# Two zero columns between prompt and sample tokens in the recurrent block

## The reference, cut to what matters

```
gate_br, x_br = split(h @ w_in)
xc  = conv4(x_br)                     # per feature: taps at t-1, t, t+1, t+2, zero outside the sequence
r, gi = sigmoid(xc @ w_a + b_a), sigmoid(xc @ w_i + b_i)     # block diagonal, 10 blocks of 128; two directions
a = exp(-8 r softplus(-lam));  u = sqrt(1 - a*a) * gi * xc
y_t = a_t * y_(t-1) + u_t             # a scan forwards and one backwards; the sample starts from a given state
out = ((y_fwd + y_bwd) * gelu(gate_br)) @ w_out
```

## Time and profile before

| what | us |
|---|---|
| median of 3 runs | 1550.23 (1549.12 to 1550.41) |
| the profiled execution, own time | 1546.95 |
| its span, first to last instruction | 1545.3 |
| PE busy in the span | 1509.9 (98%) |
| DVE busy | 1128.7 (73%) |
| ACT busy | 660.2 (43%) |
| GpSimd busy | 138.8 (9%) |

### The profile page before, as it was taken

How to read it: one execution, slowest core, us unless ns; L and a number is a source line. 1 busy time by engine, 2 the same in 40 slices (tenths; PEclk the granted TensorE clock), 3 DMA queues, 4 the chain that set the end, 5 groups by cost and what they waited for, 6 DMA issues and landing times.

```text
span 1545.3 us, 25482 instructions
## 1 busy us (share of the span) xinstructions
PE 1509.9 (98%) x9222; PEld 1482.9 (96%) x9222; DVE 1128.7 (73%) x1757; ACT 660.2 (43%) x953; POOL 138.8 (9%) x212
## 2 busy tenths in 40 slices
PE   8999999999979999999999999999999999999998
PEld 7999999989979999999999999998779999999998
DVE  4898888879987877789887777986997575344342
ACT  5533342369955333332343333225555553333321
POOL 0010000000120000001000000000642000000000
PEclk9999999999989999999999999999999999999999
DMA  9666666513432655667555556753222134334421
GB/s 375 232 234 220 229 246 223 193 56 118 142 109 96 219 192 187 205 216 243 165 183 184 192 190 215 254 194 114 69 82 89 49 109 150 124 134 137 150 94 41
DMA packets 68282, 257.08 MB, mean 166 GB/s; under 512 B 7585, under 2 KB 8609, under 8 KB 67969
## 3 DMA queue, kind: packets, MB, share of 16 engines
q1 hardware_dynamic: 48944, 187.57, 35.9%
q0 software_dynamic: 18512, 67.58, 13.0%
q10 hardware_dynamic: 768, 1.19, 0.2%
HBM read 253.68 MB, written 2.63 MB: 166 GB/s over the span
## 4 chain that ended last, share of the span: by engine, by line
PE 87%; DVE 7%; ACT 3%; issue 2%; DMA 0%; POOL 0%; DVEq 0%; SPq 0%; ACTq 0%
PE bank L570 25%; PE bank L572 25%; PE bank L571 25%; DVE tmp_a L1576 2%; DVE h_lo L1595 1%; DVE w_lo_sb L1488 1%; ACT w_hi_sb L1019 1%; PE wide L872 1%; PE bank L583 1%; PE bank L649 1%; DVE bcum L2062 0%; PE bank L894 0%; DVE wide L1507 0%; PE wide L681 0%; PE bank L693 0%
## 5 line engine op out<-in xcount | busy, mean ns | idle before, releaser
L1019 ACT ACTIVATE w_hi_sb<-raw 128x1024 fp32r<-128x1024 f32 (+3 forms) x308 | 344.1, 1122 | 476.6 <-PE bank L572 451.7
L570 PE MATMUL bank<-h_hi,w_hi_sb 128*128 128x384 f32 x1567 | 530.0, 338 | 3.4 <-DVE tmp_a L1700 1.3
L1488 DVE TENSOR_TENSOR w_lo_sb<-raw,w_hi_sb 128x1024 fp32r<-128x1024 f32 (+3 forms) x308 | 402.2, 1307 | 172.6 <-ACT w_hi_sb L1019 169.9
L571 PE MATMUL bank<-h_lo,w_hi_sb 128*128 128x384 f32 x1567 | 527.5, 337 | 0.0
L572 PE MATMUL bank<-h_hi,w_lo_sb 128*128 128x384 f32 x1567 | 527.4, 337 | 0.0
L570 PEld LDWEIGHTS bank<-h_hi,w_hi_sb 128*128 128x128 f32 x1567 | 295.4, 189 | 7.8 <-DVE w_lo_sb L1488 2.8
L572 PEld LDWEIGHTS bank<-h_hi,w_lo_sb 128*128 128x128 f32 x1567 | 295.3, 188 | 0.0
L571 PEld LDWEIGHTS bank<-h_lo,w_hi_sb 128*128 128x128 f32 x1567 | 295.2, 188 | 0.0
L570 PE MATMUL bank<-a_hi,w_hi_sb 128*128 128x384 f32 x704 | 236.9, 336 | 1.5 <-DVE a_lo L1711 1.5
L572 PE MATMUL bank<-a_hi,w_lo_sb 128*128 128x384 f32 x704 | 236.6, 336 | 0.0
L571 PE MATMUL bank<-a_lo,w_hi_sb 128*128 128x384 f32 x704 | 236.6, 336 | 0.0
(11 more groups left out here) (321 smaller groups left out, 1575.1 us busy)
## 6 DMA issues: line engine op xcount, KB each, us to landing
raw<-in_ffn_in SPq DMA_DIRECT2D x176, 512.0 KB, 3.6
ada_raw<-in_ada_w POOLq DMA_DIRECT2D x128, 512.0 KB, 3.5
raw<-in_ffn_out SPq DMA_DIRECT2D x64, 704.0 KB, 4.3
raw<-in_rg_in SPq DMA_DIRECT2D x20, 512.0 KB, 3.3
ada_first<-in_ada_w SPq DMA_DIRECT2D x8, 1024.0 KB, 17.5
raw<-in_rg_out SPq DMA_DIRECT2D x8, 640.0 KB, 3.8
raw<-in_gla_qk SPq DMA_DIRECT2D x8, 512.0 KB, 3.6
raw<-in_gla_v SPq DMA_DIRECT2D x8, 512.0 KB, 3.3
```

The source lines that it names most:

```text
L570: pe.matmul(out, w_hi_sb[:, slot, w], hi[k], start=start and j == 0, stop=False)
L571: pe.matmul(out, w_hi_sb[:, slot, w], lo[k], start=False, stop=False)
L1019: A(w_hi_sb[:, s, 0:w], raw[:, s, 0:w], ACT.Copy).then_inc(w_hi, 1)
L1488: V.tensor_tensor(w_lo_sb[:, s, 0:w], raw[:, s, 0:w], w_hi_sb[:, s, 0:w].bitcast(F32), ALU.subtract).then_inc(w_split, 1)
```

## The change

In the recurrent stage alone, every buffer has 386 columns in place of 384: two columns stand between the prompt and the sample, and they are zero in the input of the stage. The sample begins at column 130. Each tap is one DVE instruction over 385 or 384 columns, with the border inside the sample included; the zero columns stand for the zeros outside the sequences, and L1826 is gone. All matmuls, ACT and DVE steps of the stage, the output product among them, have two columns more. The norm writes its result to `hg_hi` and `hg_lo` (rows of 386), which GpSimd clears in the gap ahead of the stage; PE waits for that (`gap_cleared`). To make room, `rgc` lies where `reset` is, and `reset` is filled after the stage, behind GpSimd's `low_y`, instead of at the start of the program.

```diff
+GAP = 2
+TG = T + GAP
...
+        rg_slots = sb("rg_slots", [P, 4, 2, TG], F32, slot_scope)
...
+        hg_hi = sb("hg_hi", [P, DC, TG], F32R, hg_scope)
+        hg_lo = sb("hg_lo", [P, DC, TG], F32R, hg_scope)
...
+        rgc_scope = ExitStack()
+        rgc = sb("rgc", [P, 12, 2 * RC], F32, rgc_scope)
+        rgc_scope.close()
         reset = sb("reset", [P, T], F32, ctx)
...
-            pool.memset(reset[:, :], 1.0).then_inc(consts, 1)
-            pool.wait_ge(consts, 3)
-            pool.memset(reset[:, :].rearrange("p (n t) -> p n t", t=P)[:, :, 0:1], 0.0).then_inc(consts, 1)
...
                 if f == 0:
+                    pool.wait_ge(masks_made, 1)
+                    pool.memset(hg_hi[:, :, TP:TP + GAP].bitcast(F32), 0.0).then_inc(gap_cleared, 1)
+                    pool.memset(hg_lo[:, :, TP:TP + GAP].bitcast(F32), 0.0).then_inc(gap_cleared, 1)
                     for m in range(RC):
                         low_y(m)
+                    pool.wait_ge(gate_read, 4 * RC)
+                    pool.memset(reset[:, :], 1.0).then_inc(consts, 1)
+                    pool.wait_ge(consts, 3)
+                    pool.memset(reset[:, :].rearrange("p (n t) -> p n t", t=P)[:, :, 0:1], 0.0).then_inc(consts, 1)
...
-            arriving(base, range(DC), h_chunks, hhi_ready, h_ready, DC, DC - 1, bank, RING - 1)
+            pe.wait_ge(gap_cleared, 2)
+            arriving(base, range(DC), hg_chunks, hhi_ready, h_ready, DC, DC - 1, bank, RING - 1, TG)
...
-                tile(bank[out][:, 0:T], n % RING, range(DC), *h_chunks, True, True).then_inc(w_used, 1)
+                tile(bank[out][:, 0:TG], n % RING, range(DC), *hg_chunks, True, True).then_inc(w_used, 1)
...
-                out, ps = xc[:, m % 4, :], bank[X_BANK[m]][:, 0:T]
-                out3, ps3 = (v.rearrange("p (a b) -> p a b", a=NT) for v in (out, ps))
+                out, ps = xc[:, m % 4, :], bank[X_BANK[m]][:, 0:TG]
                 for k in (0, 2, 3):
                     s = k - 1
                     w = conv_w[:, m, k:k + 1]
-                    to, fr = (slice(1, P), slice(0, P - 1)) if s < 0 else (slice(0, P - s), slice(s, P))
-                    V.scalar_tensor_tensor(out3[:, :, to], ps3[:, :, fr], w, out3[:, :, to], ALU.mult, ALU.add)
-                    to = slice(2 * P, 2 * P + 1) if s < 0 else slice(2 * P - s, 2 * P)
-                    fr = slice(2 * P - 1, 2 * P) if s < 0 else slice(2 * P, 2 * P + s)
+                    to, fr = (slice(1, TG), slice(0, TG - 1)) if s < 0 else (slice(0, TG - s), slice(s, TG))
                     last = V.scalar_tensor_tensor(out[:, to], ps[:, fr], w, out[:, to], ALU.mult, ALU.add)
```

More of the change, by code:

```diff
@@ L193, in build @@
         hbuf_scope.close()
+        hg_scope = ExitStack()
+        hg_hi = sb("hg_hi", [P, DC, TG], F32R, hg_scope)
+        hg_lo = sb("hg_lo", [P, DC, TG], F32R, hg_scope)
+        rg_scope = ExitStack()
+        gate = sb("gate", [P, RC, TG], F32, rg_scope)
+        y32 = sb("y32", [P, RC, TG], F32, rg_scope)
+        xc = sb("xc", [P, 4, TG], F32, rg_scope)
+        xc_hi = sb("xc_hi", [P, 3, TG], F32R, rg_scope)
+        xc_lo = sb("xc_lo", [P, 3, TG], F32R, rg_scope)
+        rgs = sb("rgs", [P, 7, 2, TG], F32, rg_scope)
+        rg_scope.close()
+        rgy_scope = ExitStack()
+        y_hi = sb("y_hi", [P, RC, TG], F32R, rgy_scope)
+        y_lo = sb("y_lo", [P, RC, TG], F32R, rgy_scope)
+        rgy_scope.close()
+        hg_scope.close()
         out_scope = ExitStack()
@@ L198, in build @@
         mask_in = y_out[:, :, :].rearrange("p m t -> p (m t)")[:, 0:NLEV * P]
-        sb("span_all", [P, 2 * DC * T + 2 * FC * T], F32, ctx)
+        sb("span_all", [P, 2 * DC * T + 2 * FC * T + 2 * P], F32, ctx)
         extra = sb("extra", [P, 2 * D], F32, ctx)
         crow = extra[:, :].rearrange("p (c k) -> p c k", c=2)
-        a_slot = [rgs[:, j, :, :] for j in range(3)] + [tmp_a[:, :, :]]
-        s_slot = [rgs[:, j, :, :] for j in range(3, 6)] + [tmp_b[:, :, :]]
-        u_slot = [rgs[:, 6, :, :]] + [scr[:, j:j + 2, :] for j in (0, 2)]
+        a_slot = [rgs[:, j, :, :] for j in range(3)] + [rg_slots[:, 0, :, :]]
+        s_slot = [rgs[:, j, :, :] for j in range(3, 6)] + [rg_slots[:, 1, :, :]]
+        u_slot = [rgs[:, 6, :, :]] + [rg_slots[:, j, :, :] for j in (2, 3)]
         pst = extra[:, 0:2 * DV].rearrange("p (a b) -> p a b", a=2)
@@ L387, in col_major, with h_out, at_of @@
             return ap
+        def h_out(q):
+            return (hg_hi, hg_lo) if q == 1 else (h_hi, h_lo)
+        def at_of(q, g, t0):
+            return t0 + GAP if q == 1 and g else t0
         def row_major(ap, q, n):
@@ L576, in _ @@
             h_chunks = ([h_hi[:, k, :] for k in range(DC)], [h_lo[:, k, :] for k in range(DC)])
+            hg_chunks = ([hg_hi[:, k, :] for k in range(DC)], [hg_lo[:, k, :] for k in range(DC)])
             a_chunks = ([a_hi[:, k, :] for k in range(FC)], [a_lo[:, k, :] for k in range(FC)])
@@ L633, in norm, with arriving @@
                     keep_busy(6)
-            def arriving(base, ks, chunks, hi_ready, ready, n0, early=5, bank=bank, together=RING):
+            def arriving(base, ks, chunks, hi_ready, ready, n0, early=5, bank=bank, together=RING, width=T):
                 for b in range(together):
@@ L644, in arriving @@
                     for b in range(together):
-                        pe.matmul(bank[b][:, 0:T], w_hi_sb[:, b, w], chunks[0][k], start=k == 0, stop=False)
-                        pe.matmul(bank[b][:, 0:T], w_lo_sb[:, b, w], chunks[0][k], start=False, stop=False)
+                        pe.matmul(bank[b][:, 0:width], w_hi_sb[:, b, w], chunks[0][k], start=k == 0, stop=False)
+                        pe.matmul(bank[b][:, 0:width], w_lo_sb[:, b, w], chunks[0][k], start=False, stop=False)
                     pe.wait_ge(ready, n0 + k + 1)
                     for b in range(together):
-                        pe.matmul(bank[b][:, 0:T], w_hi_sb[:, b, w], chunks[1][k], start=False, stop=False)
+                        pe.matmul(bank[b][:, 0:width], w_hi_sb[:, b, w], chunks[1][k], start=False, stop=False)
                 pe.wait_ge(ready, n0 + len(ks))
                 for b in range(together):
-                    tile(bank[b][:, 0:T], b, ks[early:], *chunks, False, True, early).then_inc(w_used, 1)
+                    tile(bank[b][:, 0:width], b, ks[early:], *chunks, False, True, early).then_inc(w_used, 1)
                 for b in range(together, RING):
                     pe.wait_ge(w_split, base + b + 1)
-                    tile(bank[b][:, 0:T], b, ks, *chunks, True, True).then_inc(w_used, 1)
+                    tile(bank[b][:, 0:width], b, ks, *chunks, True, True).then_inc(w_used, 1)
             def one_tile_blocks(name, chunks, ks, hi_ready, ready, n0, early=5, together=RING):
@@ L789, in _ @@
             pe.wait_ge(rg_p, RC)
-            arriving(base, range(RC), y_chunks, rg_yhi, rg_yready, 0, RC - 2, bank[4:8])
+            arriving(base, range(RC), y_chunks, rg_yhi, rg_yready, 0, RC - 2, bank[4:8], width=TG)
             pe.wait_ge(gelu_ready, RC)
@@ L793, in _ @@
                 pe.wait_ge(w_split, base + b + 1)
-                tile(bank[b - RING][:, 0:T], b % RING, range(RC), *y_chunks, True, True).then_inc(w_used, 1)
+                tile(bank[b - RING][:, 0:TG], b % RING, range(RC), *y_chunks, True, True).then_inc(w_used, 1)
             ffn(1, 2)
@@ L1236, in centre_tap @@
                     act.wait_ge(rg_p, m - 3)
-                A(xc[:, m % 4, :], bank[X_BANK[m]][:, 0:T], ACT.Identity, bias=conv_b[:, m:m + 1],
+                A(xc[:, m % 4, :], bank[X_BANK[m]][:, 0:TG], ACT.Identity, bias=conv_b[:, m:m + 1],
                   scale=conv_w[:, m, 1:2]).then_inc(tap_ready, 1)
@@ L1254, in gates @@
                     act.wait_ge(gate_done, GATES_BEFORE[m] + dr + 1)
-                    A(bank[6 + dr][:, 0:T], bank[6 + dr][:, 0:T], ACT.Tanh, bias=rgc[:, 0, col[dr]],
+                    A(bank[6 + dr][:, 0:TG], bank[6 + dr][:, 0:TG], ACT.Tanh, bias=rgc[:, 0, col[dr]],
                       scale=0.5).then_inc(tanh_a, 1)
@@ L1261, in gates @@
                         act.wait_ge(gate_done, GATES_BEFORE[m] + 3 + dr)
-                    A(bank[4 + dr][:, 0:T], bank[4 + dr][:, 0:T], ACT.Tanh, bias=rgc[:, 1, col[dr]],
+                    A(bank[4 + dr][:, 0:TG], bank[4 + dr][:, 0:TG], ACT.Tanh, bias=rgc[:, 1, col[dr]],
                       scale=0.5).then_inc(tanh_i, 1)
@@ L1279, in gelu @@
                 act.wait_ge(w_used, base + RG_AT["b", m] + 1)
-                A(gate[:, m, :], bank[B_BANK[m]][:, 0:T], ACT.Gelu_apprx_tanh).then_inc(gelu_ready, 1)
+                A(gate[:, m, :], bank[B_BANK[m]][:, 0:TG], ACT.Gelu_apprx_tanh).then_inc(gelu_ready, 1)
             def high_y(m):
@@ L1860, in from_state @@
                 dve.wait_ge(rg_u, m + 1)
[L1861 to L1862 removed]
+                at = slice(TP + GAP, TP + GAP + 1)
+                V.scalar_tensor_tensor(u[:, 0, at], a[:, 0, at], h0[:, 0, m:m + 1],
```

(1 more changed line is left out.)

43 lines of the change are left out of this document (18 added, 25 removed).

## The result

The changed kernel takes 1571.72 us (median of 4 runs, 1569.53 to 1573.45); the kernel before, on the same chip, 1549.67 us (4 runs, 1546.84 to 1550.41). The ratio is 1.0151, 95% interval 1.0138 to 1.0163. The time is far above the range of the forecast, and the profiled executions differ as much: 1569.53 us after, 1546.95 before.

What follows compares the result with a forecast made beforehand. The prediction took PE to bound the recurrent stage until about 389 us and from 437, ACT between, with DVE's saving hidden. Terms 0.37 + 0.10 + 0.02 + 0.22 = +0.7 us gave 1550.9 us, range 1549.0 to 1554.0.

Steps and rivals of the forecast that it cites:

- the change part by part: Section costing taps, PE's and ACT's two columns, GpSimd and the tail of the recurrent stage; sum +0.7 us.
- The sum: Recurrent stage: 0.37 + 0.10 + 0.02 + 0.22 = +0.7 us, giving 1550.9 us for the median.
- one paragraph alone: Stage rows of 1544 bytes cross more 16-byte lines; at a supposed 1% on 636 PE matmuls, 1.1 us more.
- The rival that came nearest: PE in the recurrent stage: 386 columns cost like a fuller width, 1559.8 us; chance 0.13, including a like price on ACT.
- point of decision: PE's odd-width rival decides from 4.9 ns a matmul on (3.1 us over 636), a pace of 178.2 ns.
- signs of being wrong: 386-column pace over 178 ns, an ACT step grown by more than a few ns, or output product 2 us or more early.
- DVE hidden: Recurrent stage: DVE ends some 3.3 us freer, hidden behind ACT and PE, so the saving counts as 0.
- ACT: small: ACT between 389 and 436 us: two more columns cost 1.8 ns a step, 0.10 us in all.
- PE's columns: Recurrent stage matmuls: two columns cost 0.93 ns each, 0.37 us up to 389 us and 0.22 in the output product.
- the slope between two widths: PE's 384 columns at 173.3 ns and 512 at 232.9 give 0.466 ns a column, used to price 386.
- GpSimd: right: Gap clears before the stage are covered by some 15 us; filling `reset` after `low_y` delays nothing: 0.

Runs made afterwards that it cites:

- with the shift taken out: The changed kernel without its two unused 64-byte buffers (gap, rgc_gap), so activations begin 1024 bytes lower than in the kernel before: 1551.92 us, ratio 1.0018.
- Taking the repairs out by themselves: The kernel before without the 30 steps (L1826) that mend the convolution's border columns, at its own addresses and 384 columns: 1548.55 us, ratio 1.0000.

## Why the prediction was wrong

**The step that failed** is in the change part by part: the diff's allocations were costed as work (clears, loads, what queues behind them) and never as places. The sum has no term outside the recurrent stage, which takes for granted that a matmul that the diff doesn't touch keeps its 173.3 ns. It did not: the 6936 of this width outside the stage went to 176.7, for some 19 of the 22 us. The layout was looked at in one paragraph alone, and there only at row starts inside the stage, with a weight of 1.1 us. The 1% behind that weight is the prediction's own supposition and not from the page: the Trainium skill (SBUF — State Buffer, Specifications) names a penalty for a crossed line and no size of it. By the lines of 16 bytes that it gives, every such row, not every second one, would touch one line more.

**The rival that came nearest** was PE paying for the new layout, and it had the wrong mechanism: it laid the price on 386 columns, and set its point of decision at 178.2 ns. The pace in the stage stayed below that, 177.8 ns on `hg_hi` after (143 matmuls, start to start) and 176.3 with the shift taken out. The slowness was of 384-column matmuls elsewhere, which none of its signs of being wrong would have caught.

The other terms, read in the change with its shift taken out where the shift would blur them:

*DVE hidden: right.* The taps are steps of 616 and 619 ns, no L1826 is left, and a block takes 1.84 us (1.83 forecast). DVE by line and shape, after, the answer to the earlier trace rows:

```profile
L1848 DVE SCALAR_TENSOR_TENSOR xc<-bank,small,xc 128x385 f32<-128x385 f32 x20 | 12.3, 616 | 3.2 <-ACT xc L1261 2.9
...
L1848 DVE SCALAR_TENSOR_TENSOR xc<-bank,small,xc 128x384 f32<-128x384 f32 x10 | 6.2, 619 | 0.3
```

and its timeline, block 0, the answer to the earlier trace rows: the third tap is over and the weight block begins at 333.52 - 331.68 = 1.84.

```profile
331.68 1.93 DVE L1848 SCALAR_TENSOR_TENSOR xc<-bank,small,xc 128x385 f32<-128x385 f32 x3 [1.66 <-ACT xc L1261]
333.52 1.22 DVE L1512 TENSOR_TENSOR w_lo_sb<-raw,w_hi_sb 128x1024 fp32r<-128x1024 f32 x1
```

DVE's busy time in the stage fell by 147.72 - 144.58 = 3.1 us (3.3 forecast), and ACT's waits from 389 to 437 us still name PE alone in their counterparts after (0.7, 0.4 and 0.4 us, by the earlier trace rows 0.7, 0.4, 0.2). Taking the repairs out by themselves gained nothing that can be measured.

*ACT: small, as forecast.* By line and shape its gate steps went from 693 to 696 and from 686 to 690 ns, its own step of the convolution from 675 to 679; 1.8 ns each was forecast, 3 to 4 came, some 0.1 us more over 57 steps.

*PE's columns: the size was off.* 176.3 ns in place of 174.3 for 386 columns; 2 ns more on 636 matmuls would be 1.3 us. With the shift taken out the profiled stage took 1.05 us more, against 0.7 forecast, within what a single stage varies. PE enters its output product 438.62 - 312.61 = 126.0 us after the mark (126.4 before: within the 0.6 us that the prediction allowed) and then needs 46.6 us for 45.1. Its entry in that kernel, on PE's timeline:

```profile
438.62 0.66 PE L666 MATMUL wide<-y_hi,w_hi_sb 128*128 128x386 f32 x1 [5.33 <-DVE w_lo_sb L1510]
```

Of those 1.5 us the pace is 240 x 3 ns = 0.7. The granted clock from 437 us to the end of the stage is 0.92 there and 0.95 before, by windows; whether that dip belongs to the change one execution does not tell.

```profile
437.00:485.20 48.20, 46.58 (x251) 46.37 (x252) 35.23 (x54) 21.96 (x32) 10.90 (x11) 0.92 0.33 113
```

The prediction took the slope between two widths whose rows both keep to boundaries and noted the doubt; the taps, whose row it took for comfort, are DVE's and say nothing of PE. (The trace does have other widths, matmuls of one column among them, but none near 386.) Nor were the two widths one series: the 512-column matmuls stream the weights against the activations, the other way round, and they don't follow the shift (232.8 ns before, 232.9 with 128 bytes, over 104 of them each).

*The rest of the +2.7 us* is not located. The profiled execution is 3.7 us longer than that of before: 1.69 of it lie ahead of the first mark and 1.05 in the stage, both within what single executions vary; none in the feed-forwards behind (281.14, 281.13 and 280.31 us); and 0.94 in the attention, which nobody touched. There PE's waits differ in one line, kernel with the shift taken out:

```profile
PE wide L894 <- DVE ebuf L2135: 2.8, 1, 2.8
```

The counterpart before is 1.6 us. But it is 2.8 too with 128 bytes ahead of `x`, where the attention takes 211.28 us, as before (211.31), so this wait alone does not make the attention longer. It takes one of two values, in kernels that differ by padding alone as well; what tips it was not pursued.

*GpSimd: right.* Its clears of the gap lie ahead of the stage's mark at 314.72 by 12 us (timeline of POOL after), and PE has no wait for them; the fill of `reset` that queues behind `low_y` delays nothing that PE needs either, since the feed-forward behind the stage takes the same 281.1 us once the shift is out:

```profile
301.88 0.13 POOL L560 MEMSET hg_hi<- 128x16 f32 x1
301.92 0.13 POOL L561 MEMSET hg_lo<- 128x16 f32 x1
```

What stays open: why the distance matters, and why 64 bytes allow two paces. By the Trainium skill (SBUF — State Buffer, SBUF: two separate sides) PE has a second, independent read port for loading weights, and never waits on anyone. By that the distance would be expected to make no difference; these runs show 176.7 ns against 173.3 for the same instructions by distance alone, and the measurement decides. Whether the two reads meet in the memory or somewhere in PE no run here shows. A version of the change with 386 columns in use and rows spaced at a multiple of 256 bytes (1792), so that every chunk keeps its distance, was not tried.

## What to carry to other kernels

When a change moves, shrinks or scopes a buffer, list which operands lie behind it and how far they move, and treat the pace of every matmul that reads them as in question, in the whole program, until a trace shows it. When a result is worse by more than the touched stage can hold, compare the same untouched instruction before and after, stage by stage: a uniform 2% on one engine at an unchanged clock is no wait, and a padding with no other change separates placement from work in one run. A kernel that is tuned to a few tenths of a per cent should fix the distance between its weights and activations by an explicit padding, so that later edits don't move it.

## What the runs showed of the hardware

The pace of these fp32 matmuls (384 columns, a new block of weights each) depends on the distance of the stationary and the moving operand in SBUF: 173.2 to 173.6 ns at four of the seven distances tried, 176.7 and 176.0 at two, with the same result at 256 bytes as at 0. Moving both operands by 128 bytes leaves the pace; moving either against the other by 128 costs some 3.2 ns, 1.8%. At one distance (64 bytes off) both paces occur in one execution, a stretch at one pace lasts up to 262 us, and in the feed-forwards the change comes where the row of matmuls is interrupted. Matmuls of 512 columns with the weights as the moving operand keep their 232.8 to 232.9 ns at 0 and at 128 bytes.
